# Three weight units of each mixer: the low part is made by GpSimd instead of VectorE

## The reference, cut to what matters

```python
def token_mixer(h, w_in, conv_w, conv_b, gate_bias, mlstm_norm_gain, w_out):
    proj = h @ w_in                                   # 1024 -> 3600
    aq, ak, av, mq, mk, mv, mo, mg = jnp.split(proj, cuts, axis=-1)
    ...
    attn_out = merge_heads(dilated_attention_mixture(aq, ak, av))    # 8 heads of 64
    qk = jax.nn.silu(lax.conv_general_dilated(concat(mq, mk), conv_w, ...) + conv_b)
    ...
    cell = mlstm(forwards) + mlstm(backwards)         # 4 heads of 128
    cell = cell * lax.rsqrt(jnp.mean(cell * cell, axis=-1, keepdims=True) + NORM_EPS)
    mlstm_out = jax.nn.sigmoid(mo) * (merge_heads(cell) * mlstm_norm_gain)
    return jnp.concatenate([attn_out, mlstm_out], axis=-1) @ w_out
```

## Time and profile before

| | before |
|---|---|
| median of 3 runs | 2122.51 us (2121.04 to 2124.31) |
| the profiled execution | 2121.16 us, span 2119.2 us |
| TensorE (PE) busy | 2089.1 us, 99% of the span |
| VectorE (DVE) busy | 1570.2 us, 74% |
| ScalarE (ACT) busy | 1021.7 us, 48% |
| GpSimd (POOL) busy | 108.4 us, 5% |
| low parts, line 1518 | 349 seen, 797.0 us, mean 2.289 us |
| high parts, line 1152 to w_hi | 349 seen, 665.1 us, mean 1.911 us |
| the first mixer | about 1262 to 1409 us of the span |
| the second mixer | about 1780 to 1927 us |

### The profile page before, as it was taken

The page is one execution under the profiler, slowest core; times in us unless marked ns, Lnnn a source line. Parts: engine busy times, 40 slices in busy tenths (PEclk is TensorE's granted clock), DMA queues, the critical chain, the costliest instruction groups (busy, mean ns, idle before and its releaser), DMA issues.

```text
span 2119.2 us, 26519 instructions
## 1 busy us (share of the span) xinstructions
PE 2089.1 (99%) x10434; PEld 1744.2 (82%) x10434; DVE 1570.2 (74%) x2478; ACT 1021.7 (48%) x1172; POOL 108.4 (5%) x239
## 2 busy tenths in 40 slices
PE   7999999999999999999999999999999999999998
PEld 6988877888978889888888888778888888878887
DVE  5788768775578866788778766888768875788874
ACT  4454445444564444454454444754445444565442
POOL 0010010000010000000010000010000000001000
PEclk9999999999999999999999999999999999999999
DMA  8477646756456556565557555346556755535662
GB/s 272 164 235 228 197 161 197 212 194 199 140 178 189 189 176 202 178 218 185 193 199 230 186 178 176 118 153 206 186 172 220 231 190 188 158 101 171 197 190 88
DMA packets 291179, 394.39 MB, mean 186 GB/s; under 512 B 9956, under 2 KB 257044, under 8 KB 290928
## 3 DMA queue, kind: packets, MB, share of 16 engines
q1 hardware_dynamic: 284032, 368.22, 53.4%
q10 hardware_dynamic: 4032, 14.68, 2.1%
q0 software_dynamic: 2992, 9.81, 1.6%
HBM read 391.60 MB, written 2.12 MB: 186 GB/s over the span
## 4 chain that ended last, share of the span: by engine, by line
PE 91%; DVE 6%; ACT 1%; issue 1%; POOL 0%; DMA 0%; SPq 0%; POOLq 0%; DVEq 0%; ACTq 0%
PE psum L541 27%; PE psum L542 26%; PE psum L543 26%; PE psum L571 2%; PE psum L568 2%; PE psum L575 2%; DVE w_lo L1518 1%; PE psum L664 1%; ACT squares L1178 1%; PE psum L635 1%; PE psum L1029 0%; DVE X L1994 0%; PE psum L1057 0%; DVE Y L1545 0%; DMA raw<-in_conv_w_in 0%
## 5 line engine op out<-in xcount | busy, mean ns | idle before, releaser
L1518 DVE TENSOR_TENSOR w_lo<-raw,w_hi 128x2048 fp32r<-128x2048 f32 x349 | 797.0, 2289 | 216.3 <-ACT w_hi L1152 214.0
L1152 ACT ACTIVATE w_hi<-raw 128x2048 fp32r<-128x2048 f32 x349 | 665.1, 1911 | 185.0 <-PE psum L543 132.4
L541 PE MATMUL psum<-w_hi,xT 128*128 128x512 f32 (+1 forms) x1424 | 556.2, 391 | 1.0 <-DVE xT L1698 1.0
L542 PE MATMUL psum<-w_lo,xT 128*128 128x512 f32 (+1 forms) x1424 | 551.6, 387 | 0.0
L543 PE MATMUL psum<-w_hi,xT 128*128 128x512 f32 (+1 forms) x1424 | 551.1, 387 | 0.0
L1569 DVE STREAM_TRANSPOSE h_turned<-h_full 32x128 f32<-32x128 f32 x1024 | 310.1, 303 | 15.3
L541 PEld LDWEIGHTS psum<-w_hi,xT 128*128 128x128 f32 x1424 | 267.5, 188 | 61.2 <-issue 4.2
L543 PEld LDWEIGHTS psum<-w_hi,xT 128*128 128x128 f32 x1424 | 267.8, 188 | 55.8
L542 PEld LDWEIGHTS psum<-w_lo,xT 128*128 128x128 f32 x1424 | 267.9, 188 | 54.2
L541 PE MATMUL psum<-w_hi,h_hi 128*128 128x512 f32 x768 | 303.6, 395 | 0.0
L542 PE MATMUL psum<-w_lo,h_hi 128*128 128x512 f32 x768 | 301.5, 393 | 0.0
(11 more groups left out here) (230 smaller groups left out, 1780.5 us busy)
## 6 DMA issues: line engine op xcount, KB each, us to landing
raw<-in_ffn_w_in SPq DMA_DIRECT2D x176, 512.0 KB, 4.9
raw<-in_ffn_w_gate SPq DMA_DIRECT2D x88, 512.0 KB, 4.0
raw<-in_ffn_w_up SPq DMA_DIRECT2D x88, 512.0 KB, 5.0
raw<-in_ffn_w_down SPq DMA_DIRECT2D x44, 1024.0 KB, 4.9
raw<-in_ffn_w_out SPq DMA_DIRECT2D x44, 1024.0 KB, 4.9
raw<-in_conv_w_in SPq DMA_DIRECT2D x20, 1024.0 KB, 5.9
raw<-in_mix_w_in SPq DMA_DIRECT2D x16, 1024.0 KB, 5.4
raw<-in_mix_w_in SPq DMA_DIRECT2D x24, 512.0 KB, 4.8
```

The source lines that it names most:

```text
L541: pe.matmul(dst, l_hi, r_hi, start=first, stop=False, skip_group_check=loose)
L542: pe.matmul(dst, l_hi, r_lo, start=False, stop=False, skip_group_check=loose)
L1152: return act.activation(dst, source, ACT.Copy, **kw)
L1518: dve.tensor_tensor(w_lo[u % LO_RING][:], raw[u % LO_RING][:], f32(w_hi[hi_slot[u]][:]), ALU.subtract).then_inc(lo_ready, 1)
```

## The change

Units 9, 11 and 13 of each mixer get their low part from GpSimd. A new plan, `plan_low`, says for each unit who makes it and which count shows that it is there: `lo_by_pool` for those six units, `lo_ready` for all others, which now runs behind the unit's number by the units of GpSimd before it. VectorE's `advance` skips the six. GpSimd makes the three of a mixer one after another, behind the DMAs of the decay rows and ahead of its wait for the cell's sums. TensorE's waits, and three waits of GpSimd for `lo_ready`, take the new counts.

```diff
+LOW_BY_POOL = (9, 11, 13)
+def plan_low(stages):
+
+    by_pool = [st["kind"] == "mix" and n in LOW_BY_POOL for st in stages for n in range(COUNT[st["kind"]])]
+    return by_pool, [sum(by_pool[:u + 1]) if by_pool[u] else u + 1 - sum(by_pool[:u]) for u in range(len(by_pool))]
...
+    low_by_pool, low_count = plan_low(stages)
...
+        lo_by_pool = sem("lo_by_pool")
...
             def unit_there(u, k):
 
-                pe.wait_ge(lo_ready, u + 1)
+                pe.wait_ge(lo_by_pool if low_by_pool[u] else lo_ready, low_count[u])
...
             def advance(to):
                 while cursor[0] < min(to, total_units):
-                    split(cursor[0])
+                    if not low_by_pool[cursor[0]]:
+                        split(cursor[0])
                     cursor[0] += 1
...
+            def low_part(u):
+
+                pool.wait_ge(hi_ready, u + 1)
+                pool.tensor_tensor(w_lo[u % LO_RING][:], raw[u % LO_RING][:], w_hi[hi_slot[u]][:].bitcast(F32),
+                                   ALU.subtract).then_inc(lo_by_pool, 1)
...
                 elif st["kind"] == "mix":
                     decay_exponents()
+                    for n in LOW_BY_POOL:
+                        low_part(st["u0"] + n)
                     pool.wait_ge(cell_ready, seen.next(cell_ready))
...
-                            pool.wait_ge(lo_ready, stages[1]["u0"] + 3 * (hd + 1))
+                            pool.wait_ge(lo_ready, low_count[stages[1]["u0"] + 3 * (hd + 1) - 1])
...
-                        pool.wait_ge(lo_ready, stages[st["n"] + 1]["u0"] + QUIET_UNIT)
+                        pool.wait_ge(lo_ready, low_count[stages[st["n"] + 1]["u0"] + QUIET_UNIT - 1])
```

More of the change, by code:

```diff
@@ L710, in part @@
                             pe.matmul(dst, xT_lo[:, k, rows], hi[:, n, :], start=False, stop=False)
-                        pe.wait_ge(lo_ready, v + 1)
+                        pe.wait_ge(lo_ready, low_count[v])
                         for n, k in enumerate(ks):
```

## The result

| | before | after |
|---|---|---|
| median | 2122.55 us (2121.04 to 2124.31) | 2145.93 us (2145.09 to 2148.95) |
| ratio to before | | 1.0113, 95% interval 1.0098 to 1.0127 |
| the profiled execution | 2121.16 us, span 2119.2 | 2148.95 us, span 2146.8 |

The kernel became 23.4 us slower. I had said 11, with a range up to 2140. The lock that I argued for is there, and it costs about what I said at two of the three units. The third place, which I priced at nothing, costs most, and TensorE's clock takes a share that the sum did not have.

The account below looks back on a forecast made before the run. TensorE was taken as the bound, waiting a little for VectorE. Holds at units 9, 11 and 13 cost 3.6 + 1.9 + 0 = 5.5 us a mixer, 11.0 in all, on a median of 2122.51: 2133 us, range 2122 to 2140.

Parts of the forecast that it names:

- The lock that I argued for: A GpSimd instruction reading SBUF holds VectorE's instructions with two SBUF inputs for its whole length; 2132 us with it, 2120 without.
- unit 9, the wait: GpSimd holds the second rope_c multiplication, so line 1861 starts late and all of it lands on TensorE: +3.6 us.
- unit 11: GpSimd goes first, 1336.1 to 1340.9; line 1861 starts 2.6 us later, 0.7 of it spare: +1.9 us a mixer.
- unit 13: GpSimd enters after line 1606's last convolution step; line 1861 is 2.0 us late against TensorE's own 1.9: 0.
- TensorE bounds, and waits for VectorE, not for w_lo: In the mixers TensorE sets the time; its waits are out_lo 1.8, a_prob 0.5 and Y 0.5 us, none for w_lo.
- The hold: Time one GpSimd subtraction keeps the port: 4.8 us, two passes of 2.4 us at the small memsets' 1.17 ns an element.
- the entry at the seam of rope_c: At unit 9 GpSimd gets in between the two rope_c multiplications at 1317.72; the second waits to 1322.5.
- without a lock: Rival: GpSimd's reads do not hold VectorE, line 1861 starts earlier and the recorded waits vanish: 2120.4 us; chance 0.13.
- with a late entry: Rival: at unit 9 GpSimd gets in only after aqk, at 1318.8; 3.8 us a mixer, 2130 us; chance 0.10.
- The clock at nothing: The sum held no loss from TensorE's clock, since the 1.8 us wait left it at 1.00 before.
- the rival of the long hold: Hold of 7.2 us, 12.7 us a mixer, 2148 us; waits of 4 us could lower the clock; 0.08 with more collisions.
- Nothing gives it back: The 11.0 us lost in the two mixers stay lost, since TensorE is the bound in the stages behind as well.

## Why the prediction was right in kind and wrong in size

| a mixer, us | predicted | profiled |
|---|---|---|
| unit 9, the wait | 3.6 | 3.25 |
| unit 9, clock behind it | not in the sum | 3.05 (1.5 in some other profiles) |
| unit 11 | 1.9 | 1.36 |
| unit 13 | 0 | 4.70 |
| clock behind out_lo | not in the sum | 1.54 |
| sum | 5.5 | 13.9 |

- **TensorE bounds, and waits for VectorE, not for w_lo**: right. The new count costs nothing, and GpSimd's queue neither: no wait of TensorE for GpSimd is in the table of waits.
- **The hold**, 4.8 us by two passes at the memset's rate: 4.59 to 4.65 measured. The rate was wrong: a pure write of 2048 elements takes 1.81 us, not 2.4, so the subtraction is two and a half of them. The Trainium skill (GPSIMD Engine Reference, Performance versus the Vector engine) has 4497 ns, 2 to 3% below the six measured. With it the sum would have been 9.8, as the prediction says, no nearer.
- **The lock works on VectorE as on GpSimd**: right, and the entry at the seam of rope_c as well. The rivals without a lock and with a late entry are out by the 5.14 us of line 1815. The Trainium skill (SBUF — State Buffer, Who interferes with whom) says that whichever starts first keeps the pair; the traces agree in both directions, 1.83 us for GpSimd's small mean in the earlier trace rows and 4.13 to 5.19 for VectorE's instructions here.
- **Unit 9 and unit 11**: right in place, their waits 0.35 and 0.5 us too high. I gave unit 11 nothing beyond its own step; made alone by GpSimd it also lengthens step 11, by 0.95 and 2.57 us.
- **Unit 13 at 0 is the step that failed.** I let the high part come at 1355.9 and GpSimd get in when the pair ending at 1356.3 was over. But this pair has a seam as rope_c has, near 1355.9: by my own rule of entry the two cases were a few hundredths of a microsecond apart, and one costs 4.7 us more. With the pair from 1355.4, I had the high part 0.5 us behind its start; in the kernel after it came 0.2 behind it (1361.42 against 1361.21), ahead of the seam. ScalarE follows TensorE, which unit 11 shifted by 1.36 us where I said 1.9; VectorE was shifted by 2.3 (8.37 less the 6.07 of unit 9) where I said 2.6. So the high part came 0.25 us earlier against VectorE. The wait for conv_sum, which moves only this entry, gave back 8.2 us. I took the middle of a race for its outcome; a term like that needs both ends in the range: 5.5 + 4.7 is 10.2 a mixer, 2143.
- **The clock at nothing** is the second step that failed. It was named only in the rival of the long hold, for waits of 4 us and more. Behind the wait of 3.5 us it fell (3.05 us lost), and in the profiled execution of after also behind the wait of 1.8 (1.54 us), where that of before stayed at 1.00. Taking it for safe from one profiled execution was the mistake.
- **Nothing gives it back**: right.

The late steps explain the whole of the profiled difference. Why the other executions are some 3 us shorter than the profiled one is argued, not shown: if unit 9's clock term is 1.5 us in them instead of 3.05, as it is in both mixers of two other profiled kernels (units 9 and 13; the wait for conv_sum), that makes 3.1.

## What to carry to other kernels

Work moved from VectorE to GpSimd that reads SBUF is not moved beside VectorE's work but in front of it: price it at the whole length of the GpSimd instruction, put on VectorE's next instruction with two SBUF inputs, and ask who waits for that one. If it must be moved, choose the place by a wait (2137.7 against 2145.9 us here) or cut the instruction into short ones (2128.8), rather than leave the entry to a race of a quarter of a microsecond. And first look at the largest wait of the engine that bounds: letting half an output product start ahead of two waits that it did not need, with VectorE's new order, brought 6.6 us, where the offload could have brought 2.

## What was new about the hardware

- GpSimd gets in at the seam between two queued VectorE instructions in all the traces shown here (1317.36, 1355.39, 1361.50), and the held instruction shows as busy, 5.14 and 5.19 us for pairs of 0.75 and 0.88.
- A GpSimd instruction that only writes, 1.81 us for 128x2048, held nothing beside the same pair, which took its 0.75 us.
- The granted clock averaged 0.66 over ten microseconds behind a TensorE wait of 3.5 us, which cost 3.05 us more; four unused matmuls in the wait kept it at 1.00. Behind the same wait in other profiles it averaged 0.83 and cost 1.5 us.
- Behind a wait of 1.8 us it fell (0.83 in after, 1.5 us lost) or stayed at 1.00, in one profiled execution even one in each mixer. What tells these apart stays open.
